# One decoder layer on one core: stage entries, sums of squares, the last tile and a few hooks put elsewhere

## The chip, the core and the metric

The kernel runs on one core of one Trainium2 chip. PE multiplies matrices (PEld is its weight load), DVE and ACT are the vector and the scalar engine, POOL has a small part at the start, and SP issues the DMAs that bring weights in and results out. The metric is the device time of one execution in microseconds (us); less is better.

## What is computed

One layer of a decoder for 512 tokens of width 1024, batch 1, all in fp32.

```python
h = rmsnorm(x, g_mix)
q_sb, k_sb, v_sb, q_r, k_r, v_r, g_r, gate_sb, gate_ret = split_cols(h @ w_in)
...
merged = (jax.nn.sigmoid(gate_sb) * (y_sb @ w_branch_sb)
          + jax.nn.sigmoid(gate_ret) * (y_r @ w_branch_ret))
x = x + merged @ w_out

h = rmsnorm(x, g_ffn)
up = h @ w_up
a, u = up[..., :D_FF], up[..., D_FF:]
a = causal_depthwise_conv(a, conv_w, conv_b)
x = x + (jax.nn.gelu(a) * u) @ w_down

gate = jax.nn.sigmoid(rmsnorm(x, g_ple) @ w_ple_gate)
x = x + gate * (p_i @ w_ple_proj)
```

`y_sb` is the output of eight heads of a causal "stick-breaking" attention, `y_r` that of eight heads of retention, each head normalised by its own root mean square. `rmsnorm` needs the mean square of a token over its 1024 features.

## The kernel before

Features lie on the 128 partitions and tokens on the free axis, so a row of x is eight tiles of 128x512. Every fp32 matrix product is done as three passes on rounded parts: an operand is split into a high part (`hi`, `w_hi`, a rounding copy on ACT) and a low part (`lo`, `w_lo`, the remainder, a subtraction on DVE), and PE adds high by high (L360), low by high (L361) and high by low (L362) into one bank. A tile of 128 output features over 1024 inputs is a chunk of 8 k-steps with 3 matmuls each.

The order of work on each engine is written out by hand, and engines wait for each other by semaphores. The stages are: four pairs of heads (9 chunks of `w_in` each, in a loop from pair 1 on, with the attention and retention steps hung in as hooks between k-steps; `places[s, k]` puts a hook behind k-step k of chunk s); merge (gates and branches); out (8 tiles, `w_out`); up (44 tiles, `w_up`); down (8 tiles of 22 k-steps, `w_down`); and the gate stage `ple` (for each of 8 output tiles a gate tile of 8 k-steps on `w_pg` and a projection tile of 2 k-steps on `w_pp`).

Weights pass through a ring of three buffers. For chunk c, SP loads `w_f` once chunk c - 3 has its low part; `high` on ACT makes `w_hi` once PE is done with chunk c - 3 (`s_used`) and the load has landed; `low` on DVE makes `w_lo` (`s_wlo`), for which PE waits. Output tiles take turns in three PSUM banks `dense0` to `dense2`; `aty` is another three banks (`misc` is its first, `ybank` its third).

Places that matter below:

- `residual(n)` in out and down. DVE adds the bank to x (`s_read`); ACT squares x into `A_SQR`, then rounds the scaled x to `hi` (`s_rehi`); DVE makes its `lo` (`s_relo`) and adds the square to `A_ACC` (`s_acc`). The first tile of the next stage has k-steps that each wait for one `s_relo`. For the last tile (n = 7) both engines first do their weight work for two chunks ahead, `high` and `low` of UP0 + 2 or PLE0 + 2, and then the residual.
- The last merge tile. DVE makes the low part of chunk OUT0 + 2 and then `branch(7, 1)`, `merge(7, 1)`; ACT rounds (`high_merged`), DVE makes the low part, and k-step 7 of the first out tile waits for it.
- `stat_res`. Behind k-step 7 of the next stage's first tile, PE multiplies a matrix of ones with `A_ACC` as plain fp32 (L379). ACT takes logarithm and exponential (`norm_res`), and DVE's first multiply of the stage waits for that (`s_rrs`).
- The pairs. At hook (3, 3) PE transposes V (`turn_v`, L406), which waits for ACT's copy `evac(j, 2)` (L709); at (3, 5) `stat_y` sums rounded squares with `ones_r`; at (8, 0) to (8, 3) the four value steps of the pair's second head (L465, L467) start once ACT has copied the first head's result out of the bank (`y_out`, L785, `s_ysraw`). In pair 0 these four stand at (8, 1) to (8, 4). `y_square` on ACT squares y and rounds the squares (L770).
- The tail. The tiles of `ple` come as gate 0, projection 0, ... gate 7, projection 7. For each m DVE multiplies the gate tile by the root (`ple_gate`), ACT takes the sigmoid, and DVE multiplies the projection by it and adds to x (`ple_out`, `s_y`); SP stores the tile.

## Time and profile before

| | |
|---|---|
| time, median of 3 runs | 907.36 us (907.21 to 907.68) |
| the profiled execution | 907.26 us, of which 905.5 are its span |
| PE busy | 895.5 us, 99% of the span, 4092 matmuls |
| DVE busy, ACT busy | 515.8 us (57%), 399.7 us (44%) |
| chain that ended last, by engine | PE 91%, DVE 6%, ACT 2% |
| granted TensorE clock | 0.999 |
| bytes moved | 89.93 MB, 99 GB/s on average |

An engine's busy time is the union of its instructions' rows. A PE row is longer than its share of the engine, since matmuls overlap: what a matmul costs is the distance from its start to the next one's start. A row of the view of waits names the waiting engine and line, who released it, the sum, the number and the longest. In the timeline, "xN" marks N instructions merged into a row, and a bracket holds the idle time before it and its releaser.

### The profile page before, as it was taken

The page shows a single profiled execution, that of the slowest core. Times are in us where ns is not written, and L with a number is a line of the kernel's source. Part 1 is how long each engine was busy: PE and PEld are TensorE (multiplying, and loading weights), DVE is VectorE, ACT ScalarE, POOL GpSimd, SP SyncE. Part 2 cuts the span into 40 slices and gives each one's busy share as a digit, 9 for nine tenths or more (in the row PEclk, how much of TensorE's full clock was granted, in tenths as well). Part 3 has the DMA queues.
Part 4 walks back from the last instruction along what each step waited for, and adds up shares of the span by engine and source line. Part 5 has one row for each costly group of instructions (what it writes and reads, how often), then busy time and mean ns, then how long its engine had stood idle before and what let it go on. Part 6 is the DMA issues. An engine that isn't in the chain of part 4 may idle for free.

```text
span 905.5 us, 11499 instructions
## 1 busy us (share of the span) xinstructions
PE 895.5 (99%) x4092; PEld 726.9 (80%) x4092; DVE 515.8 (57%) x653; ACT 399.7 (44%) x519; POOL 18.0 (2%) x19
## 2 busy tenths in 40 slices
PE   9999999999999999999999999999999999999998
PEld 7777777777787888888787888888888888888786
DVE  7797677677676443333455556655566543333354
ACT  6656746746746532232345433333333332323431
POOL 1410000000000000000000000000000000000000
PEclk9999999999999999999999999999999999999999
DMA  7114114114114153223322322222222332322131
GB/s 287 70 45 166 48 40 168 46 38 166 52 35 152 48 207 105 83 91 104 117 93 93 116 93 93 93 103 104 94 93 93 90 101 88 105 87 93 61 140 73
DMA packets 28553, 89.93 MB, mean 99 GB/s; under 512 B 3920, under 2 KB 4960, under 8 KB 28400
## 3 DMA queue, kind: packets, MB, share of 16 engines
q1 hardware_dynamic: 27232, 85.87, 27.4%
q10 hardware_dynamic: 1072, 3.67, 1.3%
q8 instruction: 15, 0.25, 0.1%
q0 software_dynamic: 224, 0.06, 0.1%
q14 instruction: 10, 0.08, 0.0%
HBM read 84.34 MB, written 2.10 MB: 95 GB/s over the span
## 4 chain that ended last, share of the span: by engine, by line
PE 91%; DVE 6%; ACT 2%; issue 1%; DMA 1%; SPq 0%; ACTq 0%; DVEq 0%
PE dense L360 28%; PE dense L361 28%; PE dense L362 28%; PE z L417 2%; DVE fs L1102 1%; DVE lo L1105 1%; DVE w_lo L1102 1%; PE aty L448 1%; DMA fs<-in_xT 1%; DVE fs L1286 1%; PE aty L362 1%; PE aty L361 1%; PE aty L360 1%; PE aty L406 1%; ACT w_hi L677 1%
## 5 line engine op out<-in xcount | busy, mean ns | idle before, releaser
L360 PE MATMUL dense<-hi,w_hi 128*128 128x512 f32 x1168 | 462.9, 396 | 1.5 <-DVE lo L1105 0.9
L362 PE MATMUL dense<-hi,w_lo 128*128 128x512 f32 x1168 | 455.2, 390 | 0.0
L361 PE MATMUL dense<-lo,w_hi 128*128 128x512 f32 x1168 | 454.9, 390 | 0.0
L1102 DVE TENSOR_TENSOR w_lo<-w_f,w_hi 128x1024 fp32r<-128x1024 f32 (+2 forms) x160 | 185.6, 1160 | 226.1 <-ACT w_hi L677 225.5
L360 PEld LDWEIGHTS dense<-hi,w_hi 128*128 128x128 f32 x1168 | 219.3, 188 | 52.3 <-issue 4.5
L362 PEld LDWEIGHTS dense<-hi,w_lo 128*128 128x128 f32 x1168 | 219.2, 188 | 46.5
L361 PEld LDWEIGHTS dense<-lo,w_hi 128*128 128x128 f32 x1168 | 219.5, 188 | 43.2 <-issue 1.0
L677 ACT CAST w_hi<-w_f 128x1024 fp32r<-128x1024 f32 (+2 forms) x160 | 158.3, 990 | 181.6 <-PE dense L362 179.0
L662 ACT ACTIVATE fs<-fs 128x512 f32<-128x512 f32 (+2 forms) x79 | 55.4, 707 | 80.7 <-DVE fs L1102 41.5
L1102 DVE TENSOR_TENSOR fs<-fs 128x512 f32<-128x512 f32 (+2 forms) x119 | 87.7, 743 | 3.7 <-ACT fs L709 0.5
L1102 DVE TENSOR_TENSOR lo<-fs,hi 128x512 f32 (+3 forms) x65 | 49.2, 764 | 40.9 <-ACT hi L1037 20.1
L1102 DVE TENSOR_TENSOR fs<-dense,fs 128x512 f32<-128x512 f32 x82 | 56.1, 684 | 8.8 <-ACT fs L662 5.6
L1105 DVE SCALAR_TENSOR_TENSOR fs<-fs,cw 128x512 f32<-128x512 f32 x44 | 33.1, 752 | 28.0 <-ACT fs L662 25.0
L1037 ACT CAST hi<-fs 128x512 f32 (+1 forms) x22 | 13.7, 621 | 59.5 <-DVE fs L1102 59.5
L1105 DVE SCALAR_TENSOR_TENSOR lo<-fs,gain,hi 128x512 fp32r<-128x512 f32 (+1 forms) x32 | 25.4, 806 | 24.4 <-ACT hi L662 24.3
L662 ACT ACTIVATE fs<-fs,cw 128x512 f32<-128x512 f32 x22 | 17.9, 816 | 43.8 <-DVE fs L1102 43.8
L816 ACT CAST hi<-aty 128x512 fp32r<-128x512 f32 (+1 forms) x16 | 10.7, 695 | 39.5 <-PE aty L448 39.5
L1286 DVE TENSOR_TENSOR_SCAN fs<-z,mrev 128x511 f32<-128x511 f32 (+3 forms) x32 | 24.1, 804 | 3.7 <-ACT z L662 3.7
L760 ACT CAST hi<-z 128x1024 fp32r<-128x1024 f32 (+3 forms) x16 | 11.1, 694 | 29.1 <-DVE z L1102 29.1
L1105 DVE SCALAR_TENSOR_TENSOR fs<-fs,gain 128x512 f32<-128x512 f32 x16 | 11.7, 750 | 20.8 <-ACT fs L662 20.8
L662 ACT ACTIVATE fs<-aty,eps 128x512 f32<-128x512 f32 (+1 forms) x15 | 12.0, 803 | 18.6 <-PE aty L398 8.1
L1102 DVE TENSOR_TENSOR lo<-z,hi 128x1024 fp32r<-128x1024 f32 (+3 forms) x16 | 13.2, 824 | 12.2 <-ACT hi L760 12.2
(98 smaller groups left out, 436.6 us busy)
## 6 DMA issues: line engine op xcount, KB each, us to landing
w_f<-in_w_in SPq DMA_DIRECT2D x52, 512.0 KB, 3.3
w_f<-in_w_up SPq DMA_DIRECT2D x44, 512.0 KB, 3.1
w_f<-in_w_down SPq DMA_DIRECT2D x16, 512.0 KB, 3.5
w_f<-in_w_b SPq DMA_DIRECT2D x8, 512.0 KB, 3.2
w_f<-in_w_out SPq DMA_DIRECT2D x8, 512.0 KB, 3.1
w_f<-in_w_pg SPq DMA_DIRECT2D x8, 512.0 KB, 3.1
w_f<-in_w_down SPq DMA_DIRECT2D x8, 384.0 KB, 3.0
fs<-in_xT SPq DMA_DIRECT2D x4, 512.0 KB, 7.0
```

The lines of the kernel that those rows point to most:

```text
L360: mm(out, w1, x1, start=start, stop=False, skip_group_check=skip)
L361: mm(out, w1, x0, start=False, stop=False, skip_group_check=skip)
L362: return mm(out, w0, x1, start=False, stop=stop, skip_group_check=skip)
L417: ins = mm(z[:, hd, first_col:first_col + cols.stop - cols.start], wp[rows, w, i * P:(i + 1) * P], xp[rows, x, cols], start=first, stop=last)
L662: return nc.scalar.activation(out, src, func, **kw).then_inc(done, 1)
L677: nc.scalar.copy(w_hi[r][:, 0:kt, :], w_f[r][:, 0:kt, :]).then_inc(s_whi, 1)
L760: nc.scalar.copy(r_pair(hi, i), z[:, :, 0:width(i)]).then_inc(s_rahi, 1)
L816: ins = nc.scalar.copy(at_blocks(hi)[:, :, to, :], aty[:, 0:2, first:first + n].rearrange("p h (b c) -> p h b c", c=P))
L1037: nc.scalar.copy(hi[:, T_G + f, :], fs[:, A_U, :]).then_inc(s_ghi, 1)
L1102: return nc.vector.tensor_tensor(out, a, b, op).then_inc(done, 1)
L1105: return nc.vector.scalar_tensor_tensor(out=out, in0=a, scalar=scalar, in1=b, op0=op0, op1=op1).then_inc(done, 1)
L1286: nc.vector.tensor_tensor_scan(fs[:, A_CP + hd, to + skip:to + width], z[:, hd, last - skip:last - width:-1], mrev[:, skip:width], 0.0, AL ...
```

## The change

- **Stage entries.** `residual(7)` comes ahead of the weight work of its place, on ACT and on DVE; in the last merge tile DVE does `branch` and `merge` ahead of the weights. In every `residual` ACT rounds x before it squares it.
- **Sums of squares.** ACT rounds `A_ACC` into a row of `hi` (`high_acc`), DVE puts the remainder in `lo` (`low_acc`), and `stat_res` is two passes with `ones_r`. Its hook moves from behind k-step 7 of the first tile into the second tile (behind k-step 1 at up, behind k-step 0 at the gate stage). The load of the logarithm's table moves ahead of the second weight chunk.
- **Gate stage.** The loop over m = 1 to 6 is written out. The last tiles come as gate 6, gate 7, projection 6, projection 7; gate 7 has a row of its own (`A_U + 1`). Projection 7 is computed, multiplied, added and stored in two halves of 256 columns, in the second and third bank of `aty`.
- **Hooks of the pairs.** The second head's value steps stand at (8, 1) to (8, 4) in every pair. The rounding of the squares is a function of its own, `y_square_high`, and comes behind `evac(j, 2)` in pairs 1 to 3.

The diff, cut to its core:

```diff
+        def ple_place(m):
+
+            return 2 * m - (1 if m == KD - 1 else 0), 2 * m + 1 + (1 if m == KD - 2 else 0)
...
-            for m in range(KD):
-                load_ple(m)
+            for m in range(KD - 2):
+                load_pg(m)
+                load_pp(m)
                 if m >= 4:
                     store(m - 4)
-            for m in range(4, KD):
+            load_pg(6)
+            load_pg(7)
+            store(2)
+            load_pp(6)
+            load_pp(7)
+            for m in range(3, KD - 1):
                 store(m)
-            sp.wait_ge(s_out, 16 * KD)
+            for half in range(2):
+                cols = slice(half * SEQ // 2, (half + 1) * SEQ // 2)
+                sp.wait_ge(s_y, KD + half)
+                sp.dma_start(outT[KD - 1][:, cols], fs[:, A_X + KD - 1, cols]).then_inc(s_out, 16)
...
-                    later = 0
-                places[8, later] = at(sb_values, j, 1, 3)
-                places[8, later + 1] = at(sb_values, j, 1, 2)
-                places[8, later + 2] = at(sb_values, j, 1, 1)
-                places[8, later + 3] = at(sb_values, j, 1, 0)
+                for n in range(NT):
+                    places[8, 1 + n] = at(sb_values, j, 1, NT - 1 - n)
...
             def stat_res(n):
-                pe.wait_ge(s_acc, KD * n)
-                stat(C_ONES, A_ACC, s_rst)
+                pe.wait_ge(s_aclo, n)
+                mm(misc, ones_r[:, :], hi[:, t_acc(n), :], start=True, stop=False)
+                mm(misc, ones_r[:, :], lo[:, t_acc(n), :], start=False, stop=True).then_inc(s_rst, 1)
...
-            up(0, UP0 % 3, hooks={7: lambda: stat_res(1)}, before={k: (s_relo, k + 1) for k in range(KD)})
-            up(1, (UP0 + 1) % 3)
+            up(0, UP0 % 3, before={k: (s_relo, k + 1) for k in range(KD)})
+            up(1, (UP0 + 1) % 3, hooks={1: lambda: stat_res(1)})
...
             pe.wait_ge(s_plo, 1)
-            ple(0, 0, hooks={7: lambda: stat_res(2)}, before={k: (s_relo, KD + k + 1) for k in range(KD)})
-            with pe.Fori(0, 2) as it:
-                for q in range(3):
-                    ple(3 * it + (q + 1), q + 1)
-            ple(7, 7)
+            ple_tile(0, 0, KD, T_H, before={k: (s_relo, KD + k + 1) for k in range(KD)})
+            ple_tile(1, 1, PB, T_P, hooks={0: lambda: stat_res(2)})
+            for at in range(2, 2 * KD - 4):
+                ple_tile(at, at, KD if at % 2 == 0 else PB, T_H if at % 2 == 0 else T_P)
+            for m in (KD - 2, KD - 1):
+                ple_tile(ple_place(m)[0], ple_place(m)[0], KD, T_H)
+            ple_tile(ple_place(KD - 2)[1], ple_place(KD - 2)[1], PB, T_P)
+            at = ple_place(KD - 1)[1]
+            pe.wait_ge(s_wlo, PLE0 + at + 1)
+            for half in range(2):
+                cols = slice(half * SEQ // 2, (half + 1) * SEQ // 2)
+                for k in range(PB):
+                    ins = split3(aty[:, 1 + half, 0:SEQ // 2], w_hi[at % 3][:, k, :], w_lo[at % 3][:, k, :],
+                                 hi[:, T_P + k, cols], lo[:, T_P + k, cols], start=(k == 0), stop=(k == PB - 1))
+                ins.then_inc(s_used, 1)
...
             def back(j, prev):
                 evac(j, 2)
+                y_square_high(prev)
                 ahead(j, 3)
...
+            def high_acc(n):
+                act.wait_ge(s_acc, KD * n)
+                nc.scalar.copy(hi[:, t_acc(n), :], fs[:, A_ACC, :]).then_inc(s_achi, 1)
+                ln_exp_tables()
...
+            residual(OUT0 + 7, 7, G_FFN)
             high((UP0 + 2) // 3, (UP0 + 2) % 3)
-            residual(OUT0 + 7, 7, G_FFN)
+            high_acc(1)
             high((UP0 + 3) // 3, (UP0 + 3) % 3)
             norm_res(1)
...
-            low((OUT0 + 2) // 3, (OUT0 + 2) % 3)
             branch(7, 1, OUT0, 1, 1)
             merge(7, 1)
+            low((OUT0 + 2) // 3, (OUT0 + 2) % 3)
             low_merged(7, 1)
...
+            def low_acc(n):
+                dve.wait_ge(s_achi, n)
+                tt(lo[:, t_acc(n), :], fs[:, A_ACC, :], hi[:, t_acc(n), :], ALU.subtract, s_aclo)
...
+            def ple_last():
+                m, at = KD - 1, ple_place(KD - 1)[1]
+                dve.wait_ge(s_pg, KD)
+                for half in range(2):
+                    cols = slice(half * SEQ // 2, (half + 1) * SEQ // 2)
+                    x, t = fs[:, A_X + m, cols], ple_gate_row(m)[:, cols]
+                    dve.wait_ge(s_used, PLE0 + at + 1 + half)
+                    tt(t, aty[:, 1 + half, 0:SEQ // 2], t, ALU.mult, s_read)
+                    dve.wait_ge(s_read, read(PLET0 + at) + half)
+                    tt(x, x, t, ALU.add, s_y)
...
-            ple_out(KD - 1)
+            ple_gate(KD - 1)
+            ple_out(KD - 2)
+            ple_last()
```

The order on ACT from the last down tile on (`w_hi2` is chunk PLE0 + 2, `w_hi0` chunk PLE0 + 3; the rows with `fs<-fs` and `hi<-fs,gain` are the square and the high part of `residual(7)`). Before:

```order
L677 CAST w_hi2<-w_f2 128x1024 [waits s_used,s_wdma2]
L662 ACTIVATE fs<-fs 128x512 [waits s_read]
L662 ACTIVATE hi<-fs,gain 128x512
L677 CAST w_hi0<-w_f0 128x256 [waits s_used,s_wdma0]
L666 ACT_TABLE_LOAD
L662 ACTIVATE fs<-aty,eps 128x512 [waits s_rst]
L662 ACTIVATE fs<-fs 128x512 [waits s_rln]
```

After:

```order
L693 ACTIVATE hi<-fs,gain 128x512 [waits s_read]
L693 ACTIVATE fs<-fs 128x512
L708 CAST w_hi2<-w_f2 128x1024 [waits s_used,s_wdma2]
L1048 CAST hi<-fs 128x512 [waits s_acc]
L697 ACT_TABLE_LOAD
L708 CAST w_hi0<-w_f0 128x256 [waits s_used,s_wdma0]
L693 ACTIVATE fs<-aty,eps 128x512 [waits s_rst]
L693 ACTIVATE fs<-fs 128x512 [waits s_rln]
```

The weights of PLE0 + 2 went from first to third, and a rounding copy of the accumulated squares is new.

The same place on DVE (`fs<-fs,dense1` is the add of the last down tile). Before:

```order
L1102 TENSOR_TENSOR w_lo2<-w_f2,w_hi2 128x1024 [waits s_whi]
L1102 TENSOR_TENSOR fs<-fs,dense1 128x512 [waits s_used]
L1105 SCALAR_TENSOR_TENSOR lo<-fs,gain,hi 128x512 [waits s_rehi]
L1102 TENSOR_TENSOR fs<-fs 128x512 [waits s_acc,s_rsq]
L1102 TENSOR_TENSOR w_lo0<-w_f0,w_hi0 128x256 [waits s_whi]
L1102 TENSOR_TENSOR fs<-dense2,fs 128x512 [waits s_used,s_rrs]
```

After:

```order
L1143 TENSOR_TENSOR fs<-fs,dense1 128x512 [waits s_used]
L1146 SCALAR_TENSOR_TENSOR lo<-fs,gain,hi 128x512 [waits s_rehi]
L1143 TENSOR_TENSOR fs<-fs 128x512 [waits s_acc,s_rsq]
L1143 TENSOR_TENSOR w_lo2<-w_f2,w_hi2 128x1024 [waits s_whi]
L1143 TENSOR_TENSOR lo<-fs,hi 128x512 [waits s_achi]
L1143 TENSOR_TENSOR w_lo0<-w_f0,w_hi0 128x256 [waits s_whi]
L1143 TENSOR_TENSOR fs<-dense2,fs 128x512 [waits s_used,s_rrs]
```

The three steps of the last tile went ahead of the weights, and the remainder of the sum (`lo<-fs,hi`) stands behind them.

The end of the program on DVE (`fs<-denseN,fs` with `s_used` reads a PE tile). Before:

```order
L1102 TENSOR_TENSOR fs<-dense0,fs 128x512 [waits s_used,s_pg]
L1102 TENSOR_TENSOR fs<-fs 128x512 [waits s_read]
L1102 TENSOR_TENSOR fs<-dense1,fs 128x512 [waits s_y,s_used]
L1102 TENSOR_TENSOR fs<-dense2,fs 128x512 [waits s_used,s_pg]
L1102 TENSOR_TENSOR fs<-fs 128x512 [waits s_read]
```

After:

```order
L1143 TENSOR_TENSOR fs<-dense0,fs 128x512 [waits s_used]
L1143 TENSOR_TENSOR fs<-dense1,fs 128x512 [waits s_used,s_pg]
L1143 TENSOR_TENSOR fs<-fs 128x512 [waits s_read]
L1143 TENSOR_TENSOR fs<-aty,fs 128x256 [waits s_used,s_pg]
L1143 TENSOR_TENSOR fs<-fs 128x256 [waits s_read]
L1143 TENSOR_TENSOR fs<-aty,fs 128x256 [waits s_used]
L1143 TENSOR_TENSOR fs<-fs 128x256 [waits s_read]
```

Gate 7 (the first row) now stands ahead of projection 6 (the next two), and projection 7 is four rows of half the width.

## Rows read from the trace of the kernel before

**Rows 1.** Busy us in a stretch: length, PE, PEld, DVE, ACT, POOL, clock, DMA.

```profile
492.00:849.00 357.00, 357.00 (x1576) 295.60 (x1575) 186.38 (x223) 126.00 (x154) 0.00 (x0) 1.00 0.28 95
```

**Rows 2.** Waits of PE: who for whom, us in total, times, longest.

```profile
PE aty L465 <- ACT fs L785: 1.4, 4, 0.6
...
PE dense L360 <- DVE lo L1105: 0.9, 3, 0.4
...
PE aty L448 <- issue: 0.7, 1, 0.7
```

**Rows 3.** Timeline, pair 1, chunk 8: start us, us, engine, line, operation, count.

```profile
134.80 0.39 PE L362 MATMUL dense<-hi,w_lo 128*128 128x512 f32 x1
...
134.81 0.58 ACT L785 COPY fs<-aty 128x512 f32<-128x512 f32 x1
...
135.45 0.33 PE L465 MATMUL aty<-hi,lo 128*128 128x128 f32 x1 [0.26 <-ACT fs L785]
```

**Rows 4.** Timeline, pair 1, chunks 3: the turn of V and the sums.

```profile
100.87 0.58 ACT L709 COPY fs<-dense 128x512 f32<-128x512 f32 x1
...
101.07 0.39 PE L362 MATMUL dense<-hi,w_lo 128*128 128x512 f32 x1
...
101.58 0.32 PE L406 MATMUL aty<-cst,fs 128*128 128x128 f32 x1
...
104.60 0.40 PE L397 MATMUL aty<-hi,ones_r 128*128 128x512 f32 x1
...
104.83 0.40 PE L398 MATMUL aty<-lo,ones_r 128*128 128x512 f32 x1
```

**Rows 5.** Timeline, last merge tile and the first out tile's end.

```profile
441.94 1.23 DVE L1102 TENSOR_TENSOR w_lo<-w_f,w_hi 128x1024 fp32r<-128x1024 f32 x1 [1.54 <-ACT w_hi L677]
...
443.08 0.68 DVE L1102 TENSOR_TENSOR fs<-dense,fs 128x512 f32<-128x512 f32 x1
...
445.13 0.39 PE L362 MATMUL dense<-hi,w_lo 128*128 128x512 f32 x1
...
445.92 0.50 PE L360 MATMUL dense<-hi,w_hi 128*128 128x512 f32 x1 [0.40 <-DVE lo L1102]
```

**Rows 6.** Timeline, last down tile and the gate stage's entry.

```profile
845.65 1.05 ACT L677 CAST w_hi<-w_f 128x1024 fp32r<-128x1024 f32 x1 [3.08 <-PE dense L362]
...
849.13 0.71 ACT L662 ACTIVATE hi<-fs,gain 128x512 fp32r<-128x512 f32 x1
...
849.87 0.75 DVE L1105 SCALAR_TENSOR_TENSOR lo<-fs,gain,hi 128x512 fp32r<-128x512 f32 x1 [1.31 <-ACT hi L662]
...
849.93 0.39 PE L362 MATMUL dense<-hi,w_lo 128*128 128x512 f32 x1
...
850.68 0.50 PE L360 MATMUL dense<-hi,w_hi 128*128 128x512 f32 x1 [0.36 <-DVE lo L1105]
...
851.02 0.40 PE L361 MATMUL dense<-lo,w_hi 128*128 128x512 f32 x1
```

**Rows 7.** Timeline, the sum of squares behind that entry, PE.

```profile
851.49 1.02 PE L379 MATMUL aty<-fs,cst 128*128 128x512 f32 x2
...
852.58 0.39 PE L361 MATMUL dense<-lo,w_hi 128*128 128x512 f32 x1
```

**Rows 8.** Timeline, the program's last matmul and DVE steps.

```profile
901.13 0.39 PE L362 MATMUL dense<-hi,w_lo 128*128 128x512 f32 x1
...
901.62 0.69 DVE L1102 TENSOR_TENSOR fs<-dense,fs 128x512 f32<-128x512 f32 x1 [0.74 <-ACT fs L662]
...
902.35 0.69 DVE L1102 TENSOR_TENSOR fs<-fs 128x512 f32<-128x512 f32 x1
```

**Rows 9.** Timeline, a 256-column DVE step; view of DMA issues, KB, us to landing.

```profile
887.09 0.42 DVE L1102 TENSOR_TENSOR w_lo<-w_f,w_hi 128x256 fp32r<-128x256 f32 x1 [1.58 <-ACT w_hi L677]
...
out_t<-fs SPq DMA_DIRECT2D x8, 256.0 KB, 2.2
...
w_f<-in_w_pp SPq DMA_DIRECT2D x8, 128.0 KB, 2.0
```

More of the change, by code:

```diff
@@ L768, in y_square, with y_square_high @@
                 run(norm_y_pair(), fs[:, A_Y:A_Y + 2, :], ACT.Square, s_ysq)
+            def y_square_high(j):
                 act.wait_ge(s_ysq, j + 1)
@@ L957, in _ @@
             y_square(last)
+            y_square_high(last)
             act.wait_ge(s_ysadd, 2 * PAIRS)
@@ L1078, in _, with ple_ahead @@
                     high(DOWN0 // 3 + n + 2, 1, 8)
-            def ple_ahead(c):
-                if c < PLE0 + 2 * KD:
-                    high(c // 3, c % 3, PB if c % 2 else 8)
+            def ple_ahead(at):
+                high((PLE0 + at) // 3, at % 3, PB if at in (ple_place(m)[1] for m in range(KD)) else 8)
             def ple_gate(m):
-                act.wait_ge(s_read, read(PLET0 + 2 * m))
-                run(fs[:, A_U, :], fs[:, A_U, :], ACT.Sigmoid, s_pg)
-            ple_ahead(PLE0 + 2)
+                act.wait_ge(s_read, read(PLET0 + ple_place(m)[0]))
+                run(ple_gate_row(m), ple_gate_row(m), ACT.Sigmoid, s_pg)
             residual(DOWN0 + 7, 7, G_PLE)
-            ple_ahead(PLE0 + 3)
+            ple_ahead(2)
+            high_acc(2)
+            ple_ahead(3)
             norm_res(2)
@@ L1589, in _, with ple_ahead @@
                     low(DOWN0 // 3 + n + 2, 1, 8)
-            def ple_ahead(c):
-                if c < PLE0 + 2 * KD:
-                    low(c // 3, c % 3, PB if c % 2 else 8)
-            t = fs[:, A_U, :]
+            def ple_ahead(at):
+                low((PLE0 + at) // 3, at % 3, PB if at in (ple_place(m)[1] for m in range(KD)) else 8)
             def ple_gate(m):
-                dve.wait_ge(s_used, PLE0 + 2 * m + 1)
-                if m >= 1:
+                at = ple_place(m)[0]
+                dve.wait_ge(s_used, PLE0 + at + 1)
+                if 1 <= m < KD - 1:
@@ L1612, in _ @@
             residual(7, 1, G_PLE, PLE0, (DOWN0 + 7) % 3)
-            ple_ahead(PLE0 + 3)
+            ple_ahead(2)
+            low_acc(2)
+            ple_ahead(3)
             dve.wait_ge(s_rrs, 2)
             ple_gate(0)
-            for m in range(1, KD):
-                ple_ahead(PLE0 + 2 * m + 2)
+            for m in range(1, KD - 1):
+                ple_ahead(2 * m + 2)
                 ple_out(m - 1)
-                ple_ahead(PLE0 + 2 * m + 3)
+                ple_ahead(2 * m + 3)
```

46 lines of the change are left out of this document (26 added, 20 removed).

## The prediction

> **What bounds the kernel now.** The page's line on busy time comes first (in the table above): PE is busy for 99% of the span, so only about 10 us have no matmul in them. The view by stretches shows where those are not: in the up and down stages PE is busy in every microsecond, 357.00 of 357.00 us with 1576 matmuls [rows 1]. 357.00 / 1576 = 0.2265 us is the pace of a 512-column matmul, start to start; the 390 ns of a single row overlap. An edit is worth something only where the distance from one matmul's start to the next is over 0.227 us, or where it removes or adds matmul passes, or behind the last matmul. The view of waits, for PE alone, names the places: a matmul of the attention values waits four times for an ACT copy, 1.4 us in all and 0.6 at the most, and the dense matmul L360 waits three times for the low part of a tile from DVE, 0.9 us in all [rows 2] (two of the three are stage entries, one stands at the program's start; a third stage entry is in rows 5). The view counts from the modelled end of the matmul before, so each loss is a little larger than it says. I take the losses from the timeline, start to start.
>
> **Part 1: value hooks one k-step later, three pairs.** In pairs 1 to 3 the last L362 before the hook starts at 134.80 and the values matmul at 135.45, where 135.03 was due: 0.42 us lost. The row between them is the cause: the ACT copy `y_out(j, 0)` runs from 134.81 to 135.39 [rows 3]. The hook at (8, 1) lets three more dense matmuls (0.68 us) pass first, to 135.71, 0.3 us after the copy's end. The copy waits for nothing that the shift moves. The same gap stands in the other two loop pairs, at 203.5 and 272.1. Gain 3 x 0.42 = **1.27**. The first pair already has its hook at (8, 1) and keeps its wait, the 0.6 of the view. Behind the hook, the fourth value hook ends 0.68 - 0.42 = 0.26 us later; the copy `y_out(j, 1)` that waits for it starts over a microsecond after it today, so nothing is paid.
>
> **Part 2: the turn of V, and `y_square_high`.** At hook (3, 3) the L362 starts at 101.07, the transposes at 101.58 instead of 101.30: 0.28 lost, because ACT copies bank 2 out only at 100.87 to 101.45 [rows 4], behind the rounding of the squares (`y_square`'s second step, 1024 columns). The change puts that rounding behind the copy, so the copy starts earlier by the length of the rounding, about 1 us (1024 columns cost ACT 1.05 at 845.65 [rows 6]). 0.05 is usual before a transpose; I take 3 x 0.23 = **0.68**. What is late next: the rounded squares come later by the copy's 0.6, their low part ends near 102.8, and the sums `stat_y` that read them start at 104.60 [rows 4]: 1.5 us cover it. DVE's `low` for the next weights and `low_v` are queued behind that low part and move by 0.6 at most; DVE idles there and no PE row waits for them.
>
> **Part 3: stage entries.** Merge to out: the last matmul before the gap starts at 445.13, the next at 445.92, and the one behind it 0.34 later: 0.56 + 0.11 = **0.67** lost. DVE gives the weights of chunk OUT0 + 2 their low part first (1.23 us from 441.94), and adds the last branch only at 443.08 [rows 5]. With the branch first, it starts near 440.9, the merge ends near 442.3, ACT's high part at 442.9, the weights' low part at 443.5 and the tile's at 444.1, 1.2 us ahead of 445.36, where PE asks. Down to gate: the release is at 845.65, the order now ACT weights, DVE weights, add, ACT square, ACT high part (849.13, 0.71), DVE low part (849.87, 0.75), and PE starts at 850.68 instead of 850.16, then 0.34 again [rows 6]. Without weights and square ahead the same three steps (add 0.7, 0.71, 0.75, with the releases 2.25) end near 847.9, 2.2 us early. Gain 0.52 + 0.11 = **0.63**, and **0.62** at its twin, the entry from out to up near 490 us, whose wait is the same 0.36. The weights that now come second are ready near 850.0, and PE needs them at 852.7; no queue is held long enough for a load to be late. What takes the lead once the gap is gone is the new sum, next.
>
> **Part 4: sums of squares.** Today `stat` multiplies fp32 by fp32: the pair L379 starts at 851.49, and the dense L361 behind it and one L360 at 852.58 [rows 7]. Without the pair L360 would start at 851.49 and L361 at 851.72: 0.86 us. The new form is two rounded passes with `ones_r`. The kernel already does this in `stat_y`: its first two such passes start at 104.60 and 104.83, 0.23 apart [rows 4]. 0.86 - 0.46 = 0.40, twice: **0.80**. The cost is one ACT and one DVE pass (0.6 and 0.7 us) off PE's path. At the gate entry ACT goes high part (to 847.1), square (847.7), weights (848.8), rounding (849.4); DVE ends weights at 850.0 and the remainder at 850.7. PE comes to the hook, now in the second tile, at 851.5: 0.8 to 1.1 us of cover. At the up entry PE comes 0.7 later still. The table load moves into that same cover; the reciprocal root that DVE's first multiply waits for comes about when it did, and no bank is short for another 4 us.
>
> **Part 5: the tail.** The order becomes gate 6, gate 7, projection 6, projection 7 in halves. PE's own work grows by 12 short for 6 long matmuls (below 0.15 us) and is no longer what ends last. On the old clock projection 6 ends where gate 7 ended: its last matmul starts six paces before 901.13, at 899.77. DVE starts 0.49 behind such a start (901.13 to 901.62), and a dependent step costs 0.73 (901.62 to 902.35) [rows 8]. So DVE has 0.73 + 0.69 for tile 6, and then four 256-column steps of 0.42 [rows 9], three of them with 0.03 of release. Without overlap: 900.26 + 0.73 + 0.73 + 3 x 0.45 + 0.42 = 903.49. Where a step waits for nothing the next starts about 0.09 before the row's end (441.94 + 1.23 against 443.08) [rows 5]; that happens twice and gives some 903.3. Today's last add ends at 902.35 + 0.69 = 903.04: 0.2 to 0.45 **slower**, I take 0.2. The last store is half as large: 256 KB take 2.2 us, a 128 KB load 2.0 [rows 9]. I take -0.2; it could also save nothing, or twice that. The tail is worth **0.0**, between -0.2 and +0.5.
> A 256-column row lasts 0.42, not half of 0.69 [rows 8, 9], which speaks against cutting by columns. The Trainium skill says why, in VectorE: DVE Perf Modes, on the TRN2 errata: each instruction pays a fixed latency, and an fp32 tensor_tensor takes (N + 151) / 0.96 ns. By that rule the six steps are 2 x 0.691 + 4 x 0.424 = 3.08 us, an estimate, against 3.06 by the rows; the trace agrees.
>
> **The unrolled gate stage** I cost at nothing: loops of the same make run through rows 1 without a stall, so there is nothing to win, and what could be lost is the slower rival below.
>
> **Sum.** 1.27 + 0.68 + 0.67 + 0.63 + 0.62 + 0.80 = 4.67, tail 0.0. The profiled execution took 907.26 us (905.5 of span, 1.8 around it); 907.26 - 4.67 = 902.6, and the median of the runs is 0.1 above that execution: **902.7 us**, 0.51% less.
>
> **Rivals.**
> *The pair-stage gains are swallowed.* The hooks move, but the copy or the low parts behind them arrive later as well, and PE waits 0.3 to 0.4 us somewhere else in each pair. For: ACT and DVE run dense there, and the margin of part 1 is only 0.3 us. Against: besides that copy [rows 2] and the transposes' 0.28 [rows 4] the timeline of the loop pairs has a single PE gap over 0.15 us. Then 1.95 is missing: 904.7. Chance 0.11.
> *The rounded sums come late.* PE waits at the new hook for the remainder, 0.5 us each time, once it is later than 851.5. For: five steps in a row on two engines. Against: 0.8 us of cover. 903.7. Chance 0.08.
> *Less than 0.2% is left* (both of these and a tail at +0.5, or an entry that keeps its gap because DVE's release comes later than ACT's): about 905.8. Chance 0.04.
> *Slower: PE starves in the straight code.* 180 matmuls of the gate stage (six of its eight rounds) were two runs of one loop body and are now 180 of their own. The one PE wait that the view puts to "issue", 0.7 us, stands in straight code of the first pair [rows 2]. It decides from nine such waits on: 4.67 + 1.8 = 6.5 us; at ten, 907.36 - 4.67 + 7.0 = 909.7. Against: it stands alone, though that whole pair is straight code. Chance 0.03. The Trainium skill speaks against it too (Runtime: NRT & Kernel Launch, on instruction fetch: straight code is streamed ahead, taken branches are what stalls); no run here shows that mechanism.
> *More than forecast*, by faster stores: 901.9. Chance 0.02.
>
> **Numbers.** 0.72 for the forecast (its own range 902.2 to 903.4), and the rest as given. The range of 901.9 to 904.7 takes in the tail's bounds and most of the first two rivals. 0.2% of this time is 1.8 us, about what a measurement can tell from no change. Faster: 0.72 + 0.11 + 0.08 + 0.02 = 0.93; same 0.04; slower 0.03.
>
> **What would show it.** Right: PE's waits for the ACT copy fall from four to one, and those for a low part at the three stage entries are gone; the sum's passes are 0.23 apart; the last DVE steps follow each other without a PE row between, and end about 0.2 us later after projection 6 than now. Wrong: a new PE wait at either sum (part 4), at the value hooks (part 1), at `stat_y` (part 2), gaps put to "issue" behind 850 us (the slower rival), or a last store that takes well over 2.0 us.

## The result, and the profile after

The changed kernel takes **901.73 us** (median of 4 runs, 901.62 to 901.76) beside 907.32 us for the kernel before (4 runs on the same chip, 907.21 to 907.68): a ratio of 0.9937, with a 95% interval of 0.992 to 0.9955. The gain is 5.6 us, and 4.67 were forecast; the time lies 0.17 us below the lower end of the range. The sign and the places were right, and the sum was 0.9 us short. The interval, which is a gain of 4.1 to 7.3 us, would hold the forecast too; that its terms were short, and which, is read from the traces.

| | before | after |
|---|---|---|
| profiled execution (its span) | 907.26 (905.5) | 901.76 (900.0) |
| PE busy | 895.5 | 892.2 |
| DVE busy, ACT busy | 515.8, 399.7 | 516.4, 400.3 |
| last 512-column matmul ahead of the last projection starts | 899.77 | 894.34 |
| last DVE add ends | 903.04 | 897.84 |

PE lost only 3.3 us of busy time, though the span lost 5.5. Part of the gain never was busy time: it was gaps.

The view of waits, PE alone, after (engine, line, who released it, us in total, times, longest):

```profile
PE aty L526 <- DVE hi L1155: 1.5, 1, 1.5
PE aty L475 <- issue: 0.7, 1, 0.7
PE aty L492 <- ACT fs L818: 0.6, 1, 0.6
PE z L444 <- DVE fs L1327: 0.5, 1, 0.5
PE dense L387 <- DVE lo L1146: 0.3, 1, 0.3
...
```

L492 is the value matmul (L465 before): its waits for the ACT copy went from four to one, the first pair's. Of the three waits for a tile's low part [rows 2] one is left, the one at the program's start, and the third stage entry's wait, which the view before puts to another line of DVE (0.4 us, once), is gone too. All that is left, two rows of 0.2 us that are not shown among it, lies ahead of 75 us, up to the first pair's retention scores. The second row of waits put to "issue" that the slower rival needed does not exist.

Up to the last projection, and but for the steps that were moved, a matmul has the same ordinal in both kernels, so its start in the one can be set against its start in the other. The difference, place by place, is the account of the change:

| place | gained there, us | forecast |
|---|---|---|
| turn of V, three pairs | 3 x 0.33 | 3 x 0.23 |
| value hooks, three pairs | 3 x 0.50 | 3 x 0.42 |
| merge to out | 0.70 | 0.67 |
| out to up, and its sum | 1.09 | 0.62 + 0.40 |
| up and down stages | 0.00 | 0 |
| down to gate, and its sum | 1.10 | 0.63 + 0.40 |
| unrolled gate stage | 0.00 | 0 |
| tail: last add later by | -0.23 | -0.2 |
| tail: store shorter by | 0.30 | 0.2 |

PE's part is 5.43 (899.77 against 894.34); the loop pairs hold 2.50 of it, where 1.95 were forecast.

The turn of V in pair 1, after (timeline: start us, us, engine, line, operation), beside [rows 4]:

```profile
99.74 0.57 ACT L740 COPY fs<-dense 128x512 f32<-128x512 f32 x1
100.21 1.04 ACT L803 CAST hi<-fs 128x1024 fp32r<-128x1024 f32 x1
...
101.02 0.39 PE L389 MATMUL dense<-hi,w_lo 128*128 128x512 f32 x1
...
101.25 0.60 PE L433 MATMUL aty<-cst,fs 128*128 128x128 f32 x4
...
104.21 0.40 PE L424 MATMUL aty<-hi,ones_r 128*128 128x512 f32 x1
```

The copy now runs ahead of the rounding, the transposes start one pace (0.23) behind the dense matmul instead of 0.51, and the sums behind them are not late: the low part of the squares ends at 102.50 and the sums start at 104.21.

The value hook in pair 1, after, beside [rows 3]:

```profile
134.43 0.58 ACT L818 COPY fs<-aty 128x512 f32<-128x512 f32 x1
...
135.10 0.39 PE L389 MATMUL dense<-hi,w_lo 128*128 128x512 f32 x1
135.33 0.22 PE L492 MATMUL aty<-hi,lo 128*128 128x128 f32 x1
135.38 0.28 PE L494 MATMUL aty<-lo 128*128 128x128 f32 x1
```

The copy ends at 135.01, 0.32 ahead of the value matmul: the forecast margin of 0.3. What the forecast did not look at is the distance between the last two rows. It is 0.05 here. In the kernel before, the same two start at 135.45 [rows 3] and 135.61, 0.16 apart.

The gate entry, after, beside [rows 6, 7]:

```profile
841.27 0.69 DVE L1143 TENSOR_TENSOR fs<-fs,dense 128x512 f32<-128x512 f32 x1 [1.77 <-PE dense L389]
...
842.75 0.75 DVE L1146 SCALAR_TENSOR_TENSOR lo<-fs,gain,hi 128x512 fp32r<-128x512 f32 x1 [0.79 <-ACT hi L693]
...
845.36 0.68 DVE L1143 TENSOR_TENSOR lo<-fs,hi 128x512 fp32r<-128x512 f32 x1
...
847.19 0.39 PE L642 MATMUL aty<-hi,ones_r 128*128 128x512 f32 x1
...
847.65 0.39 PE L387 MATMUL dense<-hi,w_hi 128*128 128x512 f32 x1
```

The three steps of the last tile follow each other and end at 843.50. The remainder of the sum ends at 846.04 and PE asks for it at 847.19: 1.15 us of cover (0.8 to 1.1 forecast). The sum costs two paces, 0.46, from 847.19 to 847.65.

The tail, after, beside [rows 8]:

```profile
894.34 0.39 PE L389 MATMUL dense<-hi,w_lo 128*128 128x512 f32 x1
...
894.84 0.69 DVE L1143 TENSOR_TENSOR fs<-dense,fs 128x512 f32<-128x512 f32 x1 [0.74 <-ACT fs L693]
...
896.17 0.42 DVE L1143 TENSOR_TENSOR fs<-aty,fs 128x256 f32<-128x256 f32 x1
...
897.41 0.43 DVE L1143 TENSOR_TENSOR fs<-fs 128x256 f32<-128x256 f32 x1
```

From 894.34 to the end of the last add are 3.50 us; before it was 3.27 (899.77 to 903.04). From there to the end of the span are 2.13 us; before, 2.43. (The spans are 899.97 and 905.47 us before rounding; the 2.16 of the expectations goes by 900.0.) Both halves of part 5 came with the forecast sign and nearly cancel.

### The profile page after: what moved, and what is told of

It is laid out like the page before. It is cut to its first block, busy times and chain, and to the rows that moved or that the text cites. A ratio compares the mean times of both kernels' runs of the same rounds, so it can differ in the third digit from the quotient of the medians.

```text
span 900.0 us, 11499 instructions
## 1 busy us (share of the span) xinstructions
PE 892.2 (99%) x4098; PEld 727.3 (81%) x4098; DVE 516.4 (57%) x657; ACT 400.3 (44%) x521; POOL 18.0 (2%) x19
## 4 chain that ended last, share of the span: by engine, by line
PE 93%; DVE 4%; ACT 1%; DMA 1%; issue 1%; SPq 0%; DVEq 0%
PE dense L387 29%; PE dense L389 28%; PE dense L388 28%; PE z L444 2%; DVE lo L1146 1%; DVE fs L1143 1%; PE aty L475 1%; DVE w_lo L1143 1%; PE aty L389 1%; PE aty L388 1%; DVE fs L1327 1%; PE aty L387 1%; DMA fs<-in_xT 1%; PE aty L433 1%; PE aty L494 0%
## 5 line engine op out<-in xcount | busy, mean ns | idle before, releaser
L387 PE MATMUL dense<-hi,w_hi 128*128 128x512 f32 x1166 | 461.1, 395 | 0.5 <-DVE lo L1146 0.3
L388 PE MATMUL dense<-lo,w_hi 128*128 128x512 f32 x1166 | 454.2, 390 | 0.0
L387 PEld LDWEIGHTS dense<-hi,w_hi 128*128 128x128 f32 x1166 | 218.9, 188 | 50.4 <-issue 4.4
L388 PEld LDWEIGHTS dense<-lo,w_hi 128*128 128x128 f32 x1166 | 219.1, 188 | 42.9 <-issue 0.5
L1143 DVE TENSOR_TENSOR fs<-fs 128x512 f32<-128x512 f32 (+3 forms) x120 | 87.9, 738 | 3.8 <-ACT fs L740 0.5
L1143 DVE TENSOR_TENSOR lo<-fs,hi 128x512 fp32r<-128x512 f32 (+3 forms) x67 | 50.5, 761 | 41.4 <-ACT hi L1076 20.2
L693 ACT ACTIVATE hi<-fs,gain 128x512 fp32r<-128x512 f32 (+1 forms) x24 | 16.9, 721 | 33.8 <-DVE fs L1143 32.8
```

Source lines behind the costliest of these rows:

```text
L387: mm(out, w1, x1, start=start, stop=False, skip_group_check=skip)
L388: mm(out, w1, x0, start=False, stop=False, skip_group_check=skip)
L693: return nc.scalar.activation(out, src, func, **kw).then_inc(done, 1)
L1143: return nc.vector.tensor_tensor(out, a, b, op).then_inc(done, 1)
```

## Two theories of the missing 0.9 us

**Theory A.** A real wait of PE costs more than the gap one sees. The gap is the start-to-start distance over the pace; then the matmul behind a wait takes about 0.11 us longer until the next can start. The forecast counted that 0.11 at the stage entries (0.56 + 0.11) but not at the value hooks. At the turn it left 0.05 of the gap standing as "usual", which was not there.

**Theory B.** The terms of the forecast are right (0.42 and 0.23), and the rest came from somewhere else: from the parts acting together, from the pace, or from the tail.

The first four runs make one part each in the kernel before. They tell A from B by size, and show whether the parts add up. Where one chip served several kernels, the kernel before ran beside them: 907.37 us for these four (27 runs).

### One part alone: the value hooks

```diff
-                places[8, later] = at(sb_values, j, 1, 3)
-                places[8, later + 1] = at(sb_values, j, 1, 2)
-                places[8, later + 2] = at(sb_values, j, 1, 1)
-                places[8, later + 3] = at(sb_values, j, 1, 0)
+                for n in range(NT):
+                    places[8, 1 + n] = at(sb_values, j, 1, NT - 1 - n)
```

> The kernel before with one edit: the second head's four value steps stand at (8, 1) to (8, 4) in every pair. Theory A (a matmul that PE really waited for also restarts slowly: the next start is 0.11 us late, which my sum counted at the stage entries but not here): each of the three waits is worth 0.42 + 0.11 = 0.53, so PE is 1.6 us earlier at the end of the pairs, and the run takes 905.7. Theory B (the hook is worth the visible 0.42, and the rest of the surplus comes from the two pair edits acting together): 1.27 us earlier, 906.05. Rival of both (the wait turns up elsewhere): less than 1.0.

Measured: 905.74 us (905.65 to 905.87, 8 runs), ratio 0.9981 (0.997 to 0.9993), 1.63 us less. By the starts of equal matmuls 1.58 us: three steps of 0.53, 0.52 and 0.51, and a little between them. The view of waits has one L465 left (0.6 us, the first pair's), and the timeline of pair 1 shows the close pair of starts:

```profile
135.84 0.22 PE L465 MATMUL aty<-hi,lo 128*128 128x128 f32 x1
135.89 0.28 PE L467 MATMUL aty<-lo 128*128 128x128 f32 x1
```

That is 0.51 to 0.53 us a pair, not 0.42: as A has it. B falls for this part.

### One part alone: the turn of V

```diff
             def back(j, prev):
                 evac(j, 2)
+                y_square_high(prev)
                 ahead(j, 3)
```

> The kernel before with one edit: the rounding of the squares comes behind the copy of bank 2 on ACT in pairs 1 to 3. Theory A: transposes that come without a wait cost no 0.05 of their own, so each is worth 0.28 + 0.05 = 0.33; 1.0 us in all, 906.35. Theory B: 0.23 each as I put it, 0.68 in all, 906.65, and the two pair edits are worth more together than the sum of e1 and e2.

Measured: 906.20 us (906.08 to 906.36, 8 runs), ratio 0.9987 (0.9975 to 0.9998), 1.17 less. The steps are 0.33, 0.32 and 0.33, and some 0.1 more is gained in small pieces between them; 1.10 us in all. In pair 1:

```profile
101.22 0.39 PE L362 MATMUL dense<-hi,w_lo 128*128 128x512 f32 x1
...
101.45 0.60 PE L406 MATMUL aty<-cst,fs 128*128 128x128 f32 x4
...
101.80 0.48 PE L360 MATMUL dense<-hi,w_hi 128*128 128x512 f32 x1
```

From the dense matmul ahead to the one behind are 0.58 us. In the kernel before they were 101.07 [rows 4] and

```profile
101.58 0.65 PE L406 MATMUL aty<-cst,fs 128*128 128x128 f32 x4
101.98 0.48 PE L360 MATMUL dense<-hi,w_hi 128*128 128x512 f32 x1
```

0.91 apart. The difference of 0.33 has two pieces: the whole gap of 0.28 (0.51 less the pace, nothing "usual" left in it), and 0.05 in the transposes, 0.40 behind the wait and 0.35 without it.

### One part alone: the three stage entries

```diff
+            residual(OUT0 + 7, 7, G_FFN)
             high((UP0 + 2) // 3, (UP0 + 2) % 3)
-            residual(OUT0 + 7, 7, G_FFN)
...
-            low((OUT0 + 2) // 3, (OUT0 + 2) % 3)
             branch(7, 1, OUT0, 1, 1)
             merge(7, 1)
+            low((OUT0 + 2) // 3, (OUT0 + 2) % 3)
```

(and the same at the gate entry, on ACT and DVE.)

> The kernel before with the three stage entries alone: the last tile ahead of the weights on ACT and DVE, and the high part ahead of the square. The sums stay one fp32 product at their old place. By the prediction 0.67 + 0.62 + 0.63 = 1.92, 905.4. If the surplus of 0.03 to 0.07 at each entry belongs to the entry (matmuls behind a gap run at 0.231 instead of 0.227 for some two us), 2.05; if it belongs to the sums, 1.92 exactly. Rival: the square is now 0.7 us later and the fp32 product waits for it, which would leave 1.2 or less.

Measured: 905.35 us (905.24 to 905.52, 8 runs), ratio 0.9978 (0.9966 to 0.9989), 2.02 less. The steps are 0.70, 0.63 and 0.65, where the forecast has 0.67, 0.62 and 0.63. Where the forecast had counted the 0.11 behind the gap, its terms hold to 0.03. The rival in which the fp32 product waits for the later square, 1.2 or less in all, did not come.

### One part alone: the rounded sums

```diff
             def stat_res(n):
-                pe.wait_ge(s_acc, KD * n)
-                stat(C_ONES, A_ACC, s_rst)
+                pe.wait_ge(s_aclo, n)
+                mm(misc, ones_r[:, :], hi[:, t_acc(n), :], start=True, stop=False)
+                mm(misc, ones_r[:, :], lo[:, t_acc(n), :], start=False, stop=True).then_inc(s_rst, 1)
```

(with `high_acc`, `low_acc` and the later hook, but the entries in their old order.)

> The kernel before with the sums alone: rounded, two passes, hook in the second tile; the entries stay as they were, with the weights ahead of the last tile. The product is 0.40 to 0.46 cheaper twice. But the remainder is ready only at about 852.6 (last add of squares 851.2, rounding 0.65, remainder 0.7), and PE comes at 852.15: a new wait of 0.45 plus 0.11 each time. So next to nothing is left: 907.2 to 907.6. If instead the form alone decides, 906.4. This tests from which point my rival of the late sums decides.

Measured: 907.16 us (907.05 to 907.24, 8 runs), ratio 0.9997 (0.9986 to 1.0008): no difference that could be told. By the starts 0.17 us are gained: 0.36 at the up entry, less 0.19 at the gate entry. The expected wait "each time" came only once. At the up entry the sum stands one k-step later in its tile; the remainder ends at 492.15, PE comes at 492.43, and nothing is waited for. At the gate entry a new wait has come up (timeline):

```profile
851.67 0.69 DVE L1114 TENSOR_TENSOR lo<-fs,hi 128x512 fp32r<-128x512 f32 x1 [0.69 <-ACT hi L1019]
...
852.42 0.50 PE L624 MATMUL aty<-hi,ones_r 128*128 128x512 f32 x1 [0.31 <-DVE lo L1114]
```

This is the rival "the rounded sums come late", with the entry's order as the point from which it decides: with the old order the remainder ends at 852.36 and PE, due at 851.95, starts at 852.42; with the new it ends 1.15 us early. So the half of part 4 at the gate entry exists only together with part 3, at this hook; whether the hook one k-step later, as at the up entry, would do without part 3 no run tests. By the starts the four parts alone give 1.58 + 1.10 + 1.98 + 0.17 = 4.8. With the entries moved the sums are worth 0.91 (the fp32 run below), 0.74 more, which makes 5.6, against PE's 5.43 in the whole change. The parts together give no more than their sum, which leaves B no source.

## Taking parts out of the changed kernel

The next four ran on another chip, where the kernel before takes 908.03 us (7 runs, 907.49 to 908.21). With 3 runs each their times are too coarse for tenths; the traces are what is read. Traces differ already at their start: the same dense matmul that starts at 18.45 us in the changed kernel's trace starts up to 1.02 us later in the traces of this section and the next (0.32 in that of the changed kernel run again). Distances inside a trace are therefore compared, not its times of day.

### The old gate stage and tail

The loop over m, the old tile order and the whole last projection are back, and all else is as changed.

```diff
-            ple_tile(0, 0, KD, T_H, before={k: (s_relo, KD + k + 1) for k in range(KD)})
...
+            with pe.Fori(0, 2) as it:
+                for q in range(3):
+                    ple(3 * it + (q + 1), q + 1)
+            ple(7, 7)
```

> The changed kernel with the gate stage and the end of the program as they were before: the loop, gate 7 before nothing but its own projection, the last tile whole. The traces put the new tail at +0.23 on DVE (3.50 us from the last matmul of the last but one tile's place to the last add, 3.27 before) and -0.27 on the last store (2.16 against 2.43). So nothing is won or lost: 901.7, within 0.15. If the unrolled stage or the halves carry a part of the surplus of 0.8 us, it is 902.0 or more.

Measured: 902.65 us (901.99 to 902.95), ratio 0.9942 (0.992 to 0.9965), span 900.2. No step against the changed kernel appears in the gate stage, so unrolling it neither gained nor cost. From the matmul that starts at 894.34 in the changed kernel, here at 894.50, the last add ends 3.27 us later, at 897.77, and the span 2.43 behind that: 5.70 us, where the new tail has 3.50 + 2.13 = 5.63.

The largest rewrite of the diff is worth 0.07 us by the traces and nothing that the times can tell from zero. The 902.65 lies above the 902.0 from which the expectation sees a surplus in the tail, but so does the changed kernel itself on that chip (902.18, below).

### The fp32 sum in the new place

```diff
-                pe.wait_ge(s_aclo, n)
-                mm(misc, ones_r[:, :], hi[:, t_acc(n), :], start=True, stop=False)
-                mm(misc, ones_r[:, :], lo[:, t_acc(n), :], start=False, stop=True).then_inc(s_rst, 1)
+                pe.wait_ge(s_acc, KD * n)
+                stat(C_ONES, A_ACC, s_rst)
```

> The changed kernel with the sum of squares as one fp32 product again, but at the new place in the second tile; the rounding and the remainder are left out. If the form is what counts, each costs 0.86 instead of 0.45: 0.8 us more, 902.55. If a part of the gain was the place (the product behind k-step 7 of the first tile), less: 902.1.

Measured: 903.07 us (902.73 to 903.29), ratio 0.9948 (0.9925 to 0.9971). Against the changed kernel the starts fall back by 0.41 at once at each of the two sums, and by 0.45 once the next ten or twenty matmuls have run, at 0.23 instead of 0.2265; 0.91 in all (0.80 forecast). At the gate entry:

```profile
848.27 1.02 PE L406 MATMUL aty<-fs,cst 128*128 128x512 f32 x2
...
849.37 0.40 PE L388 MATMUL dense<-lo,w_hi 128*128 128x512 f32 x1
```

L388 starts 1.10 behind L406, less the 0.23 of the L387 between: 0.87 for the fp32 product, where two rounded passes take 0.46. It is the form that pays, not the place.

### The last projection whole, and the two products first

In the first kernel projection 7 is one tile of 512 columns, with one product, one add and one store, still behind gate 7 and projection 6.

```diff
-            for half in range(2):
-                cols = slice(half * SEQ // 2, (half + 1) * SEQ // 2)
+            for half in range(1):
+                cols = slice(0, SEQ)
```

> The changed kernel with the last projection whole: gate 7 still ahead of projection 6, but one multiply, one add and one store of 512 columns. DVE then has two steps of 0.69 in place of four of 0.42 and is free at 896.17, just as PE's last matmul is done (895.7 + 0.49): last add ends at 897.6 instead of 897.84, the store takes 2.43 instead of 2.16. Together 901.75, no change. If the halves do overlap usefully, it is 902.0 or more.

Measured: 902.16 us (902.03 to 902.2), ratio 0.994 (0.9917 to 0.9962), span 900.2. DVE's steps:

```profile
895.02 0.69 DVE L1140 TENSOR_TENSOR fs<-dense,fs 128x512 f32<-128x512 f32 x1 [0.74 <-ACT fs L690]
...
896.38 0.69 DVE L1140 TENSOR_TENSOR fs<-aty,fs 128x512 f32<-128x512 f32 x1
...
897.10 0.69 DVE L1140 TENSOR_TENSOR fs<-fs 128x512 f32<-128x512 f32 x1
```

895.02 to 897.79 are 2.77 us; the halves take 3.00 (894.84 to 897.84). The span then ends 2.43 later (900.22) where it ends 2.13 behind the half. Cutting costs 0.23 on DVE and gives 0.30 back on the store. The Trainium skill's fit in DMA: Bandwidth & Descriptors, on the anatomy of one DMA, about 2.0 us fixed and bytes / 436e3 us on top, gives 0.30 for the 128 KB that the last store is smaller, an estimate; the page made the fit on DMAs issued from GpSimd, and these are SP's. The trace agrees on the difference, and with 2.43 and 2.13 lies below the fit's 2.60 and 2.30 on the whole. The Trainium skill's rule in VectorE: DVE Perf Modes, on the TRN2 errata, an fp32 tensor_tensor of (N + 151) / 0.96 ns, gives 4 x 0.424 - 2 x 0.691 = 0.31 for the cut, an estimate; the trace has 0.23, since two of the small steps start 0.08 ahead of the end of the one before them, and one of the large ones 0.05.

In the second kernel the halves stay, and both products come ahead of both adds, so that no step waits for the step right before it.

```diff
+                for half, cols in enumerate(halves):
                     dve.wait_ge(s_used, PLE0 + at + 1 + half)
                     tt(t, aty[:, 1 + half, 0:SEQ // 2], t, ALU.mult, s_read)
+                for half, cols in enumerate(halves):
+                    x = fs[:, A_X + m, cols]
                     dve.wait_ge(s_read, read(PLET0 + at) + half)
```

> The changed kernel with DVE's last four steps in the order multiply, multiply, add, add. None of them then waits for the step right ahead of it, so the distances fall from 0.45 and 0.34 in turn to 0.34 each: the last add ends near 897.6, 0.2 earlier, 901.5. If the end is set by the store of the first half instead, which is issued 0.2 later, no change: 901.75.

Measured: 901.96 us (901.67 to 902.24), ratio 0.9936 (0.9914 to 0.9959), span 900.2.

```profile
895.15 0.69 DVE L1143 TENSOR_TENSOR fs<-dense,fs 128x512 f32<-128x512 f32 x1 [0.74 <-ACT fs L693]
...
896.48 0.75 DVE L1143 TENSOR_TENSOR fs<-aty,fs 128x256 f32<-128x256 f32 x2
...
897.15 0.75 DVE L1143 TENSOR_TENSOR fs<-fs 128x256 f32<-128x256 f32 x2
```

Two independent steps make one row of 0.75 instead of 0.42 + 0.03 + 0.42, and the last add ends 2.75 behind the first of these steps instead of 3.00. But the two stores now start nearly together, and the span ends 2.27 behind the last add instead of 2.13. Some 0.1 us is left, within what the run can tell.

## Testing the 0.11 directly

The changed kernel has one value wait left, in the first pair: the dense matmul ahead starts at 65.94, the value matmul at 66.95, 0.78 over the pace. Moving that hook by one k-step leaves a very short wait, by two none. If the cost behind a wait is fixed, the step from one to two is worth 0.10 of gap and 0.11 more. These ran on one chip with the kernel before (907.72 us, 8 runs, 907.43 to 908.14) and the changed kernel again.

> The changed kernel once more, beside the three that build on it. Both theories: as before on its own chip, 0.9937 of the kernel before, with the same wait of 0.6 us at the first pair's value hook.

Measured: the changed kernel 902.18 us (902.0 to 902.34, 5 runs), ratio 0.9939 (0.9925 to 0.9953). The result stands on a second chip.

```diff
+                first = 2 if prev is None else 1
                 for n in range(NT):
-                    places[8, 1 + n] = at(sb_values, j, 1, NT - 1 - n)
+                    places[8, first + n] = at(sb_values, j, 1, NT - 1 - n)
```

> The changed kernel with the first pair's value hooks at (8, 2) to (8, 5). In the changed kernel the last dense matmul ahead of that hook starts at 65.94 and the value matmul at 66.95, released by the ACT copy: 0.78 us over the pace. Moved by one k-step (0.68 us), PE comes to the hook at 66.85, 0.10 us ahead of the release: a wait is left. Theory A (a wait costs its gap and 0.11 us more behind it, however short the gap is): the 0.11 stays, all later matmuls come 0.68 us earlier. Theory B (only the gap counts): 0.68 as well; a theory in which the cost behind the gap grows with its length would give 0.75 or more. About 901.1 on the changed kernel's 901.7.

> The same hooks at (8, 3) to (8, 6): PE comes 0.58 us behind the copy's end and nothing is waited for. Theory A: the gap of 0.78 and the 0.11 behind it both go, later matmuls come 0.89 us earlier, 0.21 more than with (8, 2). Theory B: 0.78, 0.10 more than with (8, 2). If the copy out of the bank for the next pair is delayed by the later values, both gain less and a new wait for a DVE or ACT row shows in pair 1's first chunks. About 900.8 on the changed kernel's 901.7.

(The second has 3 in place of 2, and the turn behind the last value step.) Measured: 902.34 us (901.81 to 902.71, 4 runs), ratio 0.9939 (0.9923 to 0.9955), and 902.06 us (901.65 to 902.67, 4 runs), ratio 0.994 (0.9924 to 0.9955): both the same as the changed kernel. First the hook, at (8, 2) and then at (8, 3):

```profile
67.40 0.39 PE L389 MATMUL dense<-hi,w_lo 128*128 128x512 f32 x1
67.71 0.33 PE L492 MATMUL aty<-hi,lo 128*128 128x128 f32 x1
67.88 0.28 PE L494 MATMUL aty<-lo 128*128 128x128 f32 x1
```

```profile
67.32 0.39 PE L389 MATMUL dense<-hi,w_lo 128*128 128x512 f32 x1
67.55 0.22 PE L492 MATMUL aty<-hi,lo 128*128 128x128 f32 x1
67.61 0.28 PE L494 MATMUL aty<-lo 128*128 128x128 f32 x1
```

At (8, 2) the copy ends at 67.66 and PE, due at 67.63, starts at 67.71: a wait of 0.08, and behind it the full 0.17 to the next start. At (8, 3) there is no wait, and 0.06. So a wait of 0.08 costs the same 0.11 behind it as one of 0.78. From 59 to 73 us the matmuls gain 0.69 with (8, 2) and 0.88 with (8, 3); A expects 0.68 and 0.89, B 0.68 and 0.78. A holds.

What the 0.11 is stands in the rows of the weight load (PEld), which the forecast did not use. The first value matmul of pair 1, before and then after:

```profile
135.44 0.19 PEld L465 LDWEIGHTS aty<-hi,lo 128*128 128x128 f32 x1 [0.68 <-ACT fs L785]
```

```profile
135.10 0.19 PEld L492 LDWEIGHTS aty<-hi,lo 128*128 128x128 f32 x1
```

In the stream a matmul's load starts with the matmul before it (135.10, for a matmul at 135.33). Where PE waits, the load waits as well and starts only with its own matmul (135.44, for one at 135.45); the row of that matmul is then 0.11 longer (0.33 against 0.22, 0.50 against 0.39), and the next starts 0.11 later. With the hook at (8, 2) the load starts at 67.71, with its matmul; at (8, 3) at 67.33, one pace ahead. No semaphore wait is needed for it. Behind the score steps (`z`), which use 64 rows in place of 128, the dense matmul has the same late load and the same 0.34, in the changed kernel as in the one before:

```profile
103.39 0.50 PE L387 MATMUL dense<-hi,w_hi 128*128 128x512 f32 x1
103.39 0.19 PEld L387 LDWEIGHTS dense<-hi,w_hi 128*128 128x128 f32 x1 [0.37 <-issue]
...
103.73 0.40 PE L388 MATMUL dense<-lo,w_hi 128*128 128x512 f32 x1
```

There are 20 such places in either kernel, 0.33 to 0.34 to the next start, and the view of waits lists none of them. So the 0.11 belongs to the load that did not run ahead, and a wait is one way to get it. That is read from the rows; no run moves the load alone.

And yet the kernels are no faster: 901.1 and 900.8 were expected beside 901.7. The next PE wait has taken it all. The retention scores of the first pair, after and then with (8, 3):

```profile
73.83 0.69 DVE L1143 TENSOR_TENSOR lo<-fs,hi 128x512 fp32r<-128x512 f32 x1 [0.69 <-ACT hi L770]
74.06 0.39 PE L389 MATMUL dense<-hi,w_lo 128*128 128x512 f32 x1
...
74.66 0.50 PE L444 MATMUL z<-hi 64*128 64x512 f32 x2 [0.21 <-DVE lo L1143]
```

```profile
73.18 0.39 PE L389 MATMUL dense<-hi,w_lo 128*128 128x512 f32 x1
...
73.83 0.69 DVE L1150 TENSOR_TENSOR lo<-fs,hi 128x512 fp32r<-128x512 f32 x1 [0.69 <-ACT hi L777]
...
74.66 0.50 PE L444 MATMUL z<-hi 64*128 64x512 f32 x2 [1.10 <-DVE lo L1150]
```

PE comes 0.88 us earlier and starts at the same 74.66, because DVE's low part starts at the same 73.83. DVE and ACT set that time; PE's hook has no part in it. This is what the forecast's rival "the pair-stage gains are swallowed" describes; it did not happen in the loop pairs, and here, for the first pair's hook, it does.

The last kernel takes the hooks at (8, 3), the products first, and two more hooks of the first pair one k-step later:

```diff
-                              (5, 2): at(sb_turn, j, 0), (5, 7): at(sb_values, j, 0, 3), (6, 1): at(sb_scores, j, 2),
+                              (5, 3): at(sb_turn, j, 0), (5, 7): at(sb_values, j, 0, 3), (6, 2): at(sb_scores, j, 2),
```

> The changed kernel with the value hooks at (8, 3) to (8, 6) in the first pair, the first pair's first turn at (5, 3) and its third score step at (6, 2), and the last two DVE products ahead of the last two adds. By theory A 0.89 (value hooks), 0.68 of the 0.85 us that PE waits at 44.40 to 45.48 ahead of the turn, with the 0.11 behind that gap kept since 0.17 is left to wait, and 0.1 to 0.25 in the tail, which the mults-first run showed: 1.7 to 1.8 us in all, 900.0. Theory B: 0.78 + 0.68 + 0.1 to 0.25 = 1.6 to 1.7. If DVE's scan chain sets the first pair's pace, the turn's 0.68 comes back as a longer wait of the score or value steps around 52 to 66 us: 900.6.

Measured: 902.0 us (901.91 to 902.6, 5 runs), ratio 0.9937 (0.9923 to 0.9951), beside 902.18 for the changed kernel: the same. The expectation of 900.0 was wrong, and so was its fallback of 900.6. Its last sentence names one half of the reason: the waits for the turn and for the scan are gone, and new ones for DVE stand behind them. The other half is the wait at the retention scores, which takes the rest, as with (8, 3) alone.

```profile
PE z L444 <- DVE lo L1150: 1.1, 1, 1.1
...
PE aty L492 <- DVE lo L1354: 0.7, 2, 0.6
```

None of the runs gives a version that beats the changed kernel.

## Why the prediction was right or wrong, point by point

- **Part 1, value hooks.** Mechanism right: the copy was the cause, the margin of 0.3 us was there (0.32), and nothing later waited. The term was mis-sized: 3 x 0.42, measured 3 x 0.50 to 3 x 0.53. The forecast stopped at the start of the waiting matmul; the 0.11 to the one behind it stood in the same trace (135.45 to 135.61). It had counted exactly this at the stage entries. This is the step that failed, with part 2's: both put at nothing what a wait costs behind its gap.
- **Part 2, the turn.** Mechanism right, term mis-sized: 3 x 0.23, measured 3 x 0.33. "0.05 is usual before a transpose" was an allowance that no row bore out; without a wait the transposes start one pace behind. And the 0.05 behind the gap (0.40 for the four transposes against 0.35) was left out here too.
- **Part 3, entries.** 0.67, 0.63 and 0.62 against 0.70, 0.65 and 0.63 alone. Right.
- **Part 4, sums.** 0.80 against 0.91: the fp32 product costs 0.87 and leaves a slower pace behind it for a while. The cover held (1.15 us at the gate entry), and there it rests on part 3: without the entries that sum loses 0.19, while the one at the up entry keeps 0.36. The late-sum rival priced the delay right (0.5; PE is 0.47 late) but did not say that part 3 decides it, and only at one of the two sums.
- **Part 5, tail.** 0.0 against +0.07: the last add 0.23 later (0.2), the store 0.30 shorter (0.2, which was taken from a load's time and could have been nothing or twice that). That the two cancel was within the bounds given, and in part luck. A short DVE step does cost more than half of a long one, and the store made up for it.
- **Unrolled stage.** Nothing, as forecast. The slower rival had no such wait at all. (By its own figures it would have decided from ten waits on and not from nine: nine times 0.7 are 6.3, short of its 6.5. And the rival "less than 0.2%" adds up to 902.7 + 1.95 + 1.0 + 0.5 = 906.15, not 905.8.)
- **The sum.** 5.50 us of span against 4.67: part 1 is 0.23 short, part 2 0.31, the entries and sums together 0.17 (2.89 against 2.72), the tail 0.07, and 0.05 lies in small pieces, most of it at the program's start. The upper rival "more than forecast" was tied to faster stores; the unit cost of a wait, which every term shares, had no bound on its upper side, and so the range ended at 901.9.

## What to carry to other kernels

When a wait is removed, measure from the last matmul ahead of it to the second one behind it, in the same shape with and without a wait, not to the waiting matmul alone; the part behind the gap is paid even for a gap of 0.08 us, and the weight load's row shows it: it starts with its own matmul instead of with the one before. If several terms of a sum share one unit cost, an error in it adds up in one direction, and the range must hold that error on both sides. Before moving a hook away from a wait, look at the next wait: if what releases it doesn't depend on the engine that you speed up, it takes the whole gain, as it did in the first pair.

## What the runs showed of the hardware that was not expected

- A PE wait has a cost behind it that does not depend on its length. Two 128-column matmuls start 0.16 to 0.17 apart behind a wait and 0.05 to 0.06 apart without one, for waits of 0.08 as of 0.42 us; for 512-column matmuls it is 0.34 [rows 6] against 0.23, and for a run of four transposes 0.40 against 0.35.
- The cost goes with the weight load: where it starts with its own matmul and not with the one before, the next start is 0.11 late, behind the 64-row score steps (103.39 to 103.73) as behind a wait.
- Halving the last store from 256 to 128 KB shortens the time from the last add to the end of the span only from 2.43 to 2.13 us; with the two halves issued nearly together it is 2.27.
